# The norm of the short-conv heads: the same sums of squares taken in channel layout instead of token layout

## The chip, the cores and the metric

The kernel runs on one core of a Trainium2 chip. Its metric is the device time of one execution in microseconds. Five engines work side by side and meet at semaphores: PE (TensorE, matrix multiplies and transposes into PSUM), DVE (VectorE), ACT (ScalarE, functions from a loaded table), POOL (GpSimd), and SP, which only issues DMAs.

## The reference, cut to what matters

One layer of a hybrid encoder over 1024 tokens and 1024 channels, float32. The part that the change touches is the gated short convolution of the first 512 channels and its norm over 8 groups (heads) of 64 channels:

```
def group_rms_norm(y, g, n_groups):
    b, s, w = y.shape
    yf = y.astype(jnp.float32).reshape(b, s, n_groups, w // n_groups)
    yf = yf * lax.rsqrt(jnp.mean(yf * yf, axis=-1, keepdims=True) + EPS)
    return (yf.reshape(b, s, w) * g.astype(jnp.float32)).astype(y.dtype)
...
        y_conv = short_gated_conv(hc, bg, cg, w_conv[l])
        y_attn = chunked_band_attention(q, k, v, rel_bias[l])
        y = jnp.concatenate([group_rms_norm(y_conv, g_conv_out[l], CONV_GROUPS),
                             group_rms_norm(y_attn, g_attn_out[l], N_HEADS)], axis=-1)
        y = jnp.einsum('bsm,md->bsd', y, w_out[l])
```

Before it stand the pre-norm and the input projection, behind it a post-norm, the residual, and a SwiGLU feed-forward of width 2816 with norms of its own.

## The kernel before, in words

All matrix products are written out in "high" and "low" parts: ACT copies an operand to the fp32r type (high), DVE subtracts that from the original (low), and PE adds up high by high, high by low and low by high. The input projection of the first channels runs in six rounds ("front", `FRONT = 6`) of seven products each, by a scheme that trades one of eight block products for sums: `front_multiply(n, i)` is product i of round n, 12 matmuls of 512 columns. Its results meet in PSUM banks that DVE reads and adds up in a chain (`make_u2`, `make_u3`, `make_c22`, `make_c21`, `make_c12`), and product 6 writes into the bank that `make_c22` has just read. In the text "round 4, product 6" is `front_multiply(4, 6)`.

The conv output of channel block t (128 channels, two heads; t = 0 to 3) lies in channel layout: channels on the partitions, 1024 tokens along a row. Blocks 0 to 2 are normed during rounds 4 and 5 of the front, block 3 in the output projection (`down(c, ...)`, c = 0 to 7 its first pass). For each block the kernel does this:

- `square_y` / `square_conv` (ACT): the squares, into row CU.
- `conv_stats` (PE, line 1001): eight small fp32 matmuls, one for 128 tokens, with the squares as weights and a 128x2 matrix `group` of ones as columns, so that the sums of the two heads come out with the tokens on the partitions (128x16 in all).
- `conv_stats_read` (DVE, L2010), `conv_norm_factors` (POOL, a power of -1/2 on 128x16), `spread_conv` (ACT, L1467, each factor copied to 64 columns of row CR).
- `conv_norms` (PE, line 1007): eight transposes back to channel layout, and `conv_mix` / `conv_last` (DVE, L2015, L2336), which multiplies the row by them and by the gain.

Nothing reorders instructions: each engine runs its own list as written. PE's list of the front has a table `behind` that says behind which product a norm step comes. ACT's and DVE's lists of rounds 4 and 5 are written out by hand in the lines that follow `spread_conv` and `gated_round`. On SP, `store_conv(t)` waits for the finished row t, and the loads of later weights stand behind it. In the output projection DVE's table `tasks` puts `conv_last` into step c = 5, ahead of the split of the last operand row, which product c = 7 needs.

Of the kernel before, what the change touches and what calls it, by code (L numbers as in the profile page):

```python
# [48 lines left out]
def trunk_layer(nc, x, w_in, w_conv, rel_bias, g_conv_out, g_attn_out, w_out, g_pre_mix, g_post_mix,  # L49
# [71 lines left out]
    with ctx:  # L121
# [13 lines left out]
        arena_r = sb("arena_r", [P, NF * SEQ], F32R)  # L135
        misc = sb("misc", [P, 4 * BAND])
        ident = sb("ident", [P, P])
        group = sb("group", [P, 2])
        params = sb("params", [P, PAIRS, 5])
# [7 lines left out]
        var = sb("var", [P, 16])  # L147
# [95 lines left out]
        u2, u3, c22, s11, s4 = [misc[:, n * 512:(n + 1) * 512] for n in range(5)]  # L243
        s1, s2 = [o_raw[:, 4 * n:4 * n + 4, :].rearrange("p i c -> p (i c)") for n in range(2)]
# [159 lines left out]
        conv_factors = sem("conv_factors")  # L404
        conv_rs = sem("conv_rs")
        conv_stat = sem("conv_stat")
        conv_var = sem("conv_var")
# [4 lines left out]
        conv_norm = sem("conv_norm")  # L412
# [270 lines left out]
        def _(pool):  # L683
# [7 lines left out]
            nc.gpsimd.memset(group[0:HD, 0:1], 1.0).then_inc(consts_made, 1)  # L691
            pool.wait_ge(consts_made, 4)
            nc.gpsimd.memset(group[HD:P, 1:2], 1.0).then_inc(consts_made, 1)
            pool.wait_ge(consts_made, 5)

# [38 lines left out]
            def conv_norm_factors(t):  # L734

                pool.wait_ge(conv_var, t + 1)
                if t > 0:
                    pool.wait_ge(conv_rs, t)
                factors_to(crs[:, :], var[:, :], 16, conv_factors, t + 1)

# [4 lines left out]

            for t in range(PAIRS - 1):
                conv_norm_factors(t)
# [16 lines left out]
            conv_norm_factors(PAIRS - 1)  # L764

# [88 lines left out]
        def _(pe):  # L854
# [95 lines left out]
            def step(t, s):  # L950
# [16 lines left out]
                if s > 0:  # L967
                    pe.wait_ge(exp_done, unit(t, 2 * s))
                    if s in (2, 4):
                        pe.wait_ge(pT_act, tile(t, s - 1))  # L970
                    if s == 1 and t == 0:
                        pe.wait_ge(conv_mixed, PAIRS - 1)
# [23 lines left out]

            def conv_stats(bank):

                pe.wait_ge(consts_made, 5)
                for i in range(NT):  # L1000
                    last = mm(bank[:, 2 * i:2 * i + 2], row(CU, P, i * P), group[:, :], start=True, stop=True)  # L1001
                return last

            def conv_norms(bank, first, n):

                for b in range(n):
                    last = tr(bank[:, b * P:(b + 1) * P], row(CR, P, (first + b) * P), ident[:, :])  # L1007
                return last


# [107 lines left out]
            def stats(t):  # L1118

                pe.wait_ge(conv_sq, t + 1)  # L1120
                if t == 0:
                    pe.wait_ge(v_copied, NT)
                else:
                    pe.wait_ge(conv_var, t)
                conv_stats(PP[3]).then_inc(conv_stat, 1)

            def norms(t):

                pe.wait_ge(conv_rs, t + 1)
                if t > 0:  # L1130
                    pe.wait_ge(conv_mixed, t)
                conv_norms(PP[2], 0, NT).then_inc(conv_norm, 1)

            behind = {(4, 1): (stats, 0), (4, 3): (stats, 1), (4, 4): (norms, 0),
                      (5, 0): (norms, 1), (5, 1): (stats, 2), (5, 4): (norms, 2)}
            for n in range(FRONT):
                for i in FRONT_ORDER[n]:
                    front_multiply(n, i)
                    if (n, i) in behind:
                        task, t = behind[n, i]  # L1140
                        task(t)
# [57 lines left out]
            for c in range(len(PASSES) * KT):  # L1199
# [4 lines left out]
                if c == 3:  # L1204
                    pe.wait_ge(oT_read, PAIRS)
                    pe.wait_ge(conv_sq, PAIRS)
                    conv_stats(PP[3]).then_inc(conv_stat, 1)
# [6 lines left out]
                def begin(n, p=p):  # L1214
# [6 lines left out]
                    if p == 1 and n == 0:  # L1221
                        pe.wait_ge(mix_done, 1)
# [118 lines left out]
        def _(act):  # L1341
# [120 lines left out]
            def spread_conv(t):  # L1462

                act.wait_ge(conv_factors, t + 1)
                if 0 < t < LAST:
                    act.wait_ge(conv_norm, t)
                go(row(CR).rearrange("p (g d) -> p g d", d=HD),  # L1467
                   crs[:, :].rearrange("p (g o) -> p g o", o=1).broadcast_to([P, 16, HD]), ACT.Copy
                   ).then_inc(conv_rs, 1)
# [25 lines left out]
            front_copy_first(4), square_y(0)  # L1495
            front_high(5, 0), square_y(1), front_high(5, 1), front_high(5, 2), front_high(5, 3)
            spread_conv(0), front_high(5, 4), spread_conv(1), front_high(5, 6)
            front_copy_first(5), square_y(2), front_high(5, 5)
# [7 lines left out]
            first_chunk(0), spread_conv(2)  # L1506
# [191 lines left out]
            for c in range(1, NOUT):  # L1698
                if c < KT - 1:
                    split_out_w(c + 1), split_out_a(c + 1)  # L1700
                if c == 4:
                    act.wait_ge(oT_psum, PAIRS)
                    spread_conv(PAIRS - 1)
# [136 lines left out]
        def _(dve):  # L1840
# [165 lines left out]
            def conv_stats_read(t):  # L2006
                dve.wait_ge(conv_stat, t + 1)
                if t > 0:
                    dve.wait_ge(conv_factors, t)
                ts(var[:, :], PP[3][:, 0:16], 1.0 / HD, EPS, ALU.mult, ALU.add).then_inc(conv_var, 1)  # L2010

            def conv_mix(t):

                dve.wait_ge(conv_norm, t + 1)
                stt(row(CONV_ROWS[t]), PP[2], params[:, t, 3:4], row(CONV_ROWS[t]), ALU.mult, ALU.mult  # L2015
                    ).then_inc(conv_mixed, 1)
# [61 lines left out]
            conv_stats_read(0)  # L2078
# [6 lines left out]
            front_low(5, 3)  # L2085
            make_c22(4, tiles_of(row(CV), 1), 1)
            conv_stats_read(1)
            front_low(5, 4)
            make_c21(4, tiles_of(row(CV), 0), 0)
            conv_mix(0)  # L2090
# [3 lines left out]

            make_u2(5)
            conv_mix(1)
            make_u3(5)
            conv_stats_read(2)
            front_low(5, 5)
            low(1, 0, 0)  # L2100
            make_c22(5)
            conv_mix(2)
# [227 lines left out]
            def conv_last_stats(_):  # L2330
                dve.wait_ge(conv_stat, PAIRS)
                ts(var[:, :], PP[3][:, 0:16], 1.0 / HD, EPS, ALU.mult, ALU.add).then_inc(conv_var, 1)

            def conv_last(_):
                dve.wait_ge(conv_norm, PAIRS)
                stt(row(PAIRS - 1), PP[3], params[:, LAST, 3:4], row(CV), ALU.mult, ALU.mult).then_inc(mix_done, 1)  # L2336
# [8 lines left out]
            tasks = {1: [(attn_last, 0)], 3: [(conv_last_stats, 0)], 5: [(conv_last, 0)],  # L2345
# [303 lines left out]
```

## Time and profile before

| what | value |
|---|---|
| median of 3 runs | 1108.43 us (1108.36 to 1108.7) |
| the profiled execution | 1108.64 us |
| its span, first to last instruction | 1106.6 us |
| PE busy | 1096.3 us, 99% of the span |
| DVE busy | 769.2 us, 70% |
| ACT busy | 467.5 us, 42% |
| POOL busy | 160.5 us, 15% |

The profile is one execution taken by the hardware profiler; its own time is 2.0 us longer than its span. Busy times of PE are those of overlapping matmuls (one of 512 columns is recorded as 389 ns, and starts every 227 ns), so durations on PE are read as the distance from one start to the next.

### The profile page before, as it was taken

The page shows a single profiled execution, that of the slowest core. Times are in us where ns is not written, and L with a number is a line of the kernel's source. Part 1 is how long each engine was busy: PE and PEld are TensorE (multiplying, and loading weights), DVE is VectorE, ACT ScalarE, POOL GpSimd, SP SyncE. Part 2 cuts the span into 40 slices and gives each one's busy share as a digit, 9 for nine tenths or more (in the row PEclk, how much of TensorE's full clock was granted, in tenths as well). Part 3 has the DMA queues.
Part 4 walks back from the last instruction along what each step waited for, and adds up shares of the span by engine and source line. Part 5 has one row for each costly group of instructions (what it writes and reads, how often), then busy time and mean ns, then how long its engine had stood idle before and what let it go on. Part 6 is the DMA issues. An engine that isn't in the chain of part 4 may idle for free.

```text
span 1106.6 us, 16038 instructions
## 1 busy us (share of the span) xinstructions
PE 1096.3 (99%) x5653; PEld 907.9 (82%) x5653; DVE 769.2 (70%) x1270; ACT 467.5 (42%) x818; POOL 160.5 (15%) x258
## 2 busy tenths in 40 slices
PE   8999999999999999999999999999999999999997
PEld 7888887878888888888888888888888888888886
DVE  6878855455657656968787777878787777555584
ACT  6542233555555655734322232323223247444441
POOL 2300022010101220312112211211221110000031
PEclk9999999999999999999999999999999999999999
DMA  7332216300100444535546435543644689777632
GB/s 272 110 118 73 58 57 229 115 20 20 39 1 20 163 162 134 172 95 172 161 143 209 136 122 187 177 145 114 218 134 154 213 290 391 239 227 232 215 115 79
DMA packets 116182, 164.10 MB, mean 148 GB/s; under 512 B 7752, under 2 KB 73304, under 8 KB 116128
## 3 DMA queue, kind: packets, MB, share of 16 engines
q1 hardware_dynamic: 98496, 103.30, 29.2%
q0 software_dynamic: 16464, 55.89, 14.4%
q10 hardware_dynamic: 1168, 4.20, 1.0%
q8 instruction: 33, 0.54, 0.2%
q14 instruction: 21, 0.17, 0.0%
HBM read 119.56 MB, written 46.94 MB: 150 GB/s over the span
## 4 chain that ended last, share of the span: by engine, by line
PE 97%; ACT 1%; DVE 1%; DMA 1%; POOL 0%; issue 0%; SPq 0%; DVEq 0%; POOLq 0%
PE psum L1280 34%; PE psum L1307 18%; PE psum L874 12%; PE psum L1113 10%; PE psum L1164 8%; PE psum L1025 4%; PE psum L917 3%; PE psum L898 2%; PE psum L888 2%; PE psum L863 1%; PE psum L1001 1%; DMA arena<-in_x 1%; PE psum L925 0%; PE psum L1007 0%; PE psum L907 0%; ACT arena L1516 0%
## 5 line engine op out<-in xcount | busy, mean ns | idle before, releaser
L1280 PE MATMUL psum<-arena_r,ws 128*128 128x512 f32 x960 | 224.1, 389 | 0.0
L1280 PEld LDWEIGHTS psum<-arena_r,ws 128*128 128x128 f32 x960 | 180.2, 188 | 37.4
L1280 PE MATMUL psum<-hT,ws 128*128 128x512 f32 x720 | 169.9, 389 | 0.0
L1280 PEld LDWEIGHTS psum<-hT,ws 128*128 128x128 f32 x720 | 135.1, 188 | 28.0
L874 PE MATMUL psum<-hT,ws 128*128 128x512 f32 (+1 forms) x624 | 142.3, 380 | 0.4 <-ACT arena L1542 0.4
L1307 PE MATMUL psum<-hT 128*128 128x512 f32 (+1 forms) x600 | 135.2, 385 | 0.0
L1307 PEld LDWEIGHTS psum<-hT 128*128 128x128 f32 x600 | 111.3, 188 | 22.5
L874 PEld LDWEIGHTS psum<-hT,ws 128*128 128x128 f32 x624 | 107.9, 189 | 20.1 <-issue 0.8
L2411 DVE TENSOR_TENSOR misc<-misc,psum 128x512 f32<-128x512 f32 x100 | 68.5, 685 | 48.4 <-PE psum L1280 46.1
L1731 ACT ACTIVATE ws<-o_raw 128x512 fp32r<-128x512 f32 x40 | 25.1, 628 | 139.1 <-DVE o_raw L2389 138.6
L1164 PE MATMUL psum<-ws,hT 128*128 128x512 f32 x348 | 81.8, 393 | 0.0
L1307 PE MATMUL psum<-ws 128*128 128x512 f32 (+1 forms) x348 | 78.1, 382 | 0.0
L1164 PEld LDWEIGHTS psum<-ws,hT 128*128 128x128 f32 x348 | 64.5, 188 | 13.5 <-issue 0.4
L1307 PEld LDWEIGHTS psum<-ws 128*128 128x128 f32 x348 | 63.8, 188 | 12.6
L1731 ACT ACTIVATE ws<-raw 128x512 fp32r<-128x512 f32 x80 | 49.7, 623 | 39.7 <-PE psum L1280 39.3
L1113 PE MATMUL psum<-arena_r,ws 128*128 128x512 f32 x276 | 65.4, 391 | 0.0
L1113 PEld LDWEIGHTS psum<-arena_r,ws 128*128 128x128 f32 x276 | 51.4, 188 | 10.5
L2406 DVE TENSOR_TENSOR ws<-raw,ws 128x512 fp32r<-128x512 f32 x80 | 55.1, 690 | 6.6
L2485 DVE TENSOR_TENSOR hT<-arena,hT 128x512 fp32r<-128x512 f32 x62 | 40.1, 687 | 21.8 <-ACT hT L1778 21.4
L1778 ACT ACTIVATE hT<-arena 128x512 fp32r<-128x512 f32 x62 | 35.6, 624 | 38.6 <-PE psum L1307 29.8
L1357 ACT ACTIVATE misc<-arena 128x1024 bf16<-128x1024 f32 (+2 forms) x37 | 34.8, 941 | 40.3 <-DVE arena L2537 16.6
L1113 PE MATMUL psum<-hT,ws 128*128 128x512 f32 x216 | 51.2, 390 | 0.0
(264 smaller groups left out, 1563.3 us busy)
## 6 DMA issues: line engine op xcount, KB each, us to landing
raw<-in_w_ffn_in SPq DMA_DIRECT2D x44, 512.0 KB, 4.1
act_scratch<-arena POOLq DMA_DIRECT2D x77, 256.0 KB, 3.2
raw<-in_w_in SPq DMA_DIRECT2D x22, 512.0 KB, 3.8
arena<-in_w_ffn_out POOLq DMA_DIRECT2D x22, 512.0 KB, 5.7
arena<-act_scratch SPq DMA_DIRECT2D x38, 256.0 KB, 3.5
arena<-in_x SPq DMA_DIRECT2D x16, 512.0 KB, 6.4
raw<-in_w_out SPq DMA_DIRECT2D x16, 512.0 KB, 3.5
raw<-act_scratch SPq DMA_DIRECT2D x26, 256.0 KB, 3.4
```

Source lines behind the costliest of these rows:

```text
L874: last = mm(PP[pair][:, at:end] if to is None else to, w[wp], hT[:, hp, k, at:end], start=(k == 0 and (wp, hp) == (0, 0)), stop=(k == KT - ...
L1025: last = mm(v_bank(i), hT[:, hp, k, i * P:(i + 1) * P], v_weights(wp, k), start=(k == 0 and part == 0), stop=k == 7 and part == (1 if i < ...
L1113: last = mm(blocks(front_bank(n, i)), w[:, k * P:(k + 1) * P], b_operand(i, part, k), start=fresh_bank and k == 0 and w is hi and part == ...
L1164: last = mm(pair[:, half * 512:(half + 1) * 512], a, ws[:, slot, wp, half * 512:(half + 1) * 512], start=(first is not None and a is hi an ...
L1280: last = mm(blocks(bank), w[:, k * P:(k + 1) * P], b_operand(i, part, k), start=fresh_bank and k == 0 and w is hi and part == 0, stop=k == ...
L1307: last = mm(bank[:, at:end], a[:, n * P:(n + 1) * P], b[:, at:end], start=fresh_bank and a is ah and b is bh, stop=i == NP - 1 and a is al ...
L1357: go(dst, src, ACT.Square, scale=scale, accum_out=acc).then_inc(done[0], 1)
L1731: go(w_op(i)[0], w_raw[i], ACT.Copy).then_inc(w_hi, 1)
L1778: go(out_op(c, part)[0], raw_ring[c % RING][:, part * 512:(part + 1) * 512], ACT.Copy).then_inc(out_hi, 1)
L2406: tt(lo, w_raw[i], hi.bitcast(F32), ALU.subtract).then_inc(w_split, 1)
L2411: tt(out, a, bank, ALU.add).then_inc(made, 1)
L2485: tt(lo, raw_ring[c % RING][:, part * 512:(part + 1) * 512], hi.bitcast(F32), ALU.subtract).then_inc(out_split, 1)
```

## The change

The norm stays in channel layout. PE multiplies a 128x128 block matrix that holds 1/64 where row and column belong to one head by the squares, so that every channel of a head gets the head's mean, at its own place. For blocks 0 to 2 the squares are split in two fp32r parts (a high copy on ACT, a low part by subtraction on DVE), and the matmuls take both; for block 3 the matmuls are plain fp32, one for each head and half row. ACT takes the root of mean + EPS out of PSUM, DVE the reciprocal of a whole 128x1024 row, and one more DVE operation multiplies by gain and row. The read of the sums, the power on POOL, the spreading copy and the transposes go.

```
+        same_head = misc_r[:, 3 * 512:3 * 512 + P]
...
             def stats(t):
+                pe.wait_ge(conv_lo, t + 1)
                 if t > 0:
+                    pe.wait_ge(conv_root, t)
+                for half in range(2):
+                    for part in (CR, CU):
+                        last = mm(PP[2][:, half * HALF:(half + 1) * HALF], same_head, row_r(part)[:, half * HALF:(half + 1) * HALF],
+                                  start=(part == CR), stop=(part == CU))
+                last.then_inc(conv_stat, 1)
-            behind = {(4, 1): (stats, 0), (4, 3): (stats, 1), (4, 4): (norms, 0),
-                      (5, 0): (norms, 1), (5, 1): (stats, 2), (5, 4): (norms, 2)}
+            behind = {(FRONT - 2, 3): 0, (FRONT - 1, 0): 1, (FRONT - 1, 3): 2}
...
                 if c == 3:
                     pe.wait_ge(oT_read, PAIRS)
                     pe.wait_ge(conv_sq, PAIRS)
-                    conv_stats(PP[3]).then_inc(conv_stat, 1)
-                if c == 6:
-                    pe.wait_ge(conv_rs, PAIRS)
-                    conv_norms(PP[3], 0, NT).then_inc(conv_norm, 1)
+                    for half in range(2):
+                        for h in range(2):
+                            last = mm(PP[3][h * HD:(h + 1) * HD, half * HALF:(half + 1) * HALF],
+                                      group[:, h:h + 1].broadcast_to([P, HD]), row(CU, HALF, half * HALF))
+                    last.then_inc(conv_stat, 1)
...
+            def high_sq(t):
+                act.wait_ge(conv_sq, t + 1)
...
+                if t > 0:
+                    act.wait_ge(conv_mixed, t)
+                go(row_r(CR), row(CU), ACT.Copy).then_inc(conv_hi, 1)
+            def conv_roots(t, bank):
+                act.wait_ge(conv_stat, t + 1)
+                go(row(CR), bank, ACT.Sqrt, bias=eps_col[:, 0:1]).then_inc(conv_root, 1)
...
+            def low_sq(t):
+                dve.wait_ge(conv_hi, t + 1)
+                tt(row_r(CU), row(CU), row_r(CR).bitcast(F32), ALU.subtract).then_inc(conv_lo, 1)
+            def conv_mix(t, src, to):
+                dve.wait_ge(conv_root, t + 1)
+                chain(nc.vector.reciprocal(row(CR), row(CR)))
+                return stt(to, src, params[:, t, 3:4], row(CR), ALU.mult, ALU.mult)
+            def mix_row(t):
+                conv_mix(t, row(CONV_ROWS[t]), row(CONV_ROWS[t])).then_inc(conv_mixed, 1)
```

PE's list, rounds 4 and 5, before (L1113 is a product of the front, 128x2 the sums, ident the transposes):

```order
L1113 MATMUL psum<-arena_r,ws 128x512 x11
L1001 MATMUL psum<-group,arena 128x2 [waits consts_made,v_copied,conv_sq]
L1001 MATMUL psum<-group,arena 128x2 x7
L1113 MATMUL psum<-arena_r,ws 128x512 [waits c21_made,front_lo]
L1113 MATMUL psum<-arena_r,ws 128x512 x11
L1113 MATMUL psum<-hT,ws 128x512 [waits p1_copied,front_lo]
L1113 MATMUL psum<-hT,ws 128x512 x11
L1001 MATMUL psum<-group,arena 128x2 [waits consts_made,conv_var,conv_sq]
L1001 MATMUL psum<-group,arena 128x2 x7
L1113 MATMUL psum<-arena_r,ws 128x512 [waits c12_made,front_lo]
L1113 MATMUL psum<-arena_r,ws 128x512 x11
L1007 MATMUL psum<-ident,arena 128x128 [waits conv_rs]
```

The same place in the changed kernel, to the product that waits for `make_c22` (L1089 is the product, L1101 the matmuls with the block matrix):

```order
L1089 MATMUL psum<-arena_r,ws 128x512 [waits c21_made,front_lo]
L1089 MATMUL psum<-arena_r,ws 128x512 x11
L1089 MATMUL psum<-hT,ws 128x512 [waits p1_copied,front_lo]
L1089 MATMUL psum<-hT,ws 128x512 x11
L1101 MATMUL psum<-arena_r,misc_r 128x512 [waits conv_lo]
L1101 MATMUL psum<-arena_r,misc_r 128x512 x3
L1089 MATMUL psum<-arena_r,ws 128x512 [waits c12_made,front_lo]
L1089 MATMUL psum<-arena_r,ws 128x512 x11
L1089 MATMUL psum<-arena_r,ws 128x512 [waits u3_made,front_lo]
L1089 MATMUL psum<-arena_r,ws 128x512 x11
L1089 MATMUL psum<-hT,ws 128x512 [waits c22_made,front_lo]
```

The sums of block 0 have gone behind round 4's product 3, those of blocks 1 and 2 behind products 0 and 3 of round 5, and the groups of eight transposes are gone.

DVE's list at the end of round 4, before (L1996 multiplies a gate in, L1966 reads a bank, here for `make_c22` and `make_c21`, L1961 makes a low part):

```order
L1996 TENSOR_TENSOR arena<-arena,psum 128x4x128 [waits prod]
L1961 TENSOR_TENSOR ws<-raw,ws 128x512 [waits front_hi]
L1966 TENSOR_TENSOR arena<-misc,psum 128x4x128 [waits prod]
L2010 TENSOR_SCALAR var<-psum 128x16 [waits conv_factors,conv_stat,c22_made]
L1961 TENSOR_TENSOR ws<-o_raw,ws 128x512 [waits front_hi]
L1966 TENSOR_TENSOR arena<-misc,psum 128x4x128 [waits prod]
L2015 SCALAR_TENSOR_TENSOR arena<-psum,params,arena 128x1024 [waits conv_norm,c21_made]
```

And in the changed kernel:

```order
L1973 TENSOR_TENSOR arena<-arena,psum 128x4x128 [waits prod]
L1938 TENSOR_TENSOR ws<-raw,ws 128x512 [waits front_hi]
L1990 RECIPROCAL arena<-arena 128x1024 [waits conv_root]
L1991 SCALAR_TENSOR_TENSOR arena<-arena,params 128x1024 [waits dve_seq]
L1943 TENSOR_TENSOR arena<-misc,psum 128x4x128 [waits prod]
L1938 TENSOR_TENSOR ws<-o_raw,ws 128x512 [waits front_hi,c22_made]
L1985 TENSOR_TENSOR arena_r<-arena,arena_r 128x1024 [waits conv_hi]
L1943 TENSOR_TENSOR arena<-misc,psum 128x4x128 [waits prod]
```

The reciprocal of block 0 and its product with the row now stand ahead of the read for `make_c22`; before, the row was multiplied behind the read for `make_c21`.

ACT's list at the same place in the changed kernel (L1412 makes a high part, L1446 is the root, L1430 the square, L1441 the high copy of the squares):

```order
L1412 ACTIVATE ws<-raw 128x512 [waits prod,raw_landed0]
L1446 ACT_TABLE_LOAD
L1446 ACTIVATE arena<-psum,eps_col 128x1024 [waits conv_stat]
L1430 ACTIVATE arena<-arena 128x1024 [waits conv_stat,front_out]
L1412 ACTIVATE ws<-o_raw 128x512 [waits prod,s_made]
L1441 ACTIVATE arena_r<-arena 128x1024 [waits conv_mixed,conv_sq]
L1412 ACTIVATE ws<-misc 128x512 [waits prod,s_made]
```

Before, none of the table loads stood there, and the spreading copies of L1467 stood where the roots are. A fourth place is like the second: in the output projection the reciprocal of block 3 stands on DVE where L2336 stood, ahead of the two splits of step c = 6.

## Rows read from the trace of the kernel before

**Rows 1.** The page: busy time of PE, granted clock, the chain by engine.
```profile
PE 1096.3 (99%) x5653; PEld 907.9 (82%) x5653; DVE 769.2 (70%) x1270; ACT 467.5 (42%) x818; POOL 160.5 (15%) x258
...
PEclk9999999999999999999999999999999999999999
...
PE 97%; ACT 1%; DVE 1%; DMA 1%; POOL 0%; issue 0%; SPq 0%; DVEq 0%; POOLq 0%
```

**Rows 2.** Timeline of PE, rounds 3 to 5: start us, us, line, operation, count.
```profile
134.24 5.60 PE L1113 MATMUL psum<-hT,ws 128*128 128x512 f32 x24
139.68 2.88 PE L1113 MATMUL psum<-arena_r,ws 128*128 128x512 f32 x12
142.40 1.84 PE L1001 MATMUL psum<-group,arena 128*128 128x2 f32 x16
144.10 2.97 PE L1113 MATMUL psum<-arena_r,ws 128*128 128x512 f32 x12
...
183.47 2.88 PE L874 MATMUL psum<-hT,ws 128*128 128x512 f32 x12
```

**Rows 3.** Groups by line and shape, DVE: busy us, mean ns, idle us before.
```profile
L2140 DVE TENSOR_SCALAR nmax<-omax 128x1 f32<-128x1 f32 x64 | 9.8, 154 | 2.2
L2297 DVE TENSOR_TENSOR arena<-arena 128x1024 f32<-128x1024 f32 x8 | 9.8, 1224 | 0.3
...
L2593 DVE RECIPROCAL newt<-gate 128x1 f32<-128x1 f32 x1 | 0.2, 165 | 0.2 <-ACT gate L1816 0.2
...
L2591 DVE TENSOR_TENSOR newt<-ssq 128x1 f32<-128x1 f32 x1 | 0.2, 158 | 0.1
```

**Rows 4.** Timeline of ACT, round 4.
```profile
141.14 1.05 ACT L1460 ACTIVATE arena<-arena 128x1024 f32<-128x1024 f32 x1
142.09 0.62 ACT L1442 ACTIVATE ws<-raw 128x512 fp32r<-128x512 f32 x1
```

**Rows 5.** Timeline of ACT near the end: the one load of the root's table.
```profile
1085.56 1.28 ACT L1835 ACT_TABLE_LOAD   x1
1086.86 0.21 ACT L1835 ACTIVATE o_eps<-rst 128x4 f32<-128x4 f32 x1
```

**Rows 6.** Timeline of DVE, rounds 4 and 5.
```profile
142.67 0.69 DVE L1966 TENSOR_TENSOR misc<-misc,psum 128x512 f32<-128x512 f32 x1 [1.52 <-PE psum L1113]
...
147.84 0.69 DVE L1945 TENSOR_TENSOR o_raw<-raw 128x512 f32<-128x512 f32 x1
...
150.75 0.69 DVE L1961 TENSOR_TENSOR ws<-o_raw,ws 128x512 fp32r<-128x512 f32 x1
151.36 0.68 DVE L1961 TENSOR_TENSOR ws<-raw,ws 128x512 fp32r<-128x512 f32 x1
...
154.41 0.69 DVE L1966 TENSOR_TENSOR arena<-misc,psum 128x512 f32<-128x512 f32 x1 [1.17 <-PE psum L1113]
...
158.74 1.28 DVE L2015 SCALAR_TENSOR_TENSOR arena<-psum,params,arena 128x1024 f32<-128x1024 f32 x1
```

**Rows 7.** Timeline of PE in the output projection's first pass, and plain fp32 matmuls before it.
```profile
365.82 1.26 PE L917 MATMUL psum<-arena 128*64 128x128 f32 x20
...
380.65 1.84 PE L1001 MATMUL psum<-group,arena 128*128 128x2 f32 x16
382.35 12.55 PE L1164 MATMUL psum<-ws,hT 128*128 128x512 f32 x54
...
395.53 18.03 PE L1164 MATMUL psum<-ws,hT 128*128 128x512 f32 x78
```

**Rows 8.** Timeline of ACT there (L1636 copies an operand row, L1467 spreads factors).
```profile
385.38 1.04 ACT L1636 ACTIVATE hT<-arena 128x1024 fp32r<-128x1024 f32 x1
387.33 1.06 ACT L1467 ACTIVATE arena<-crs 128x1024 f32<-128x1024 f32 x1 [0.90 <-POOL crs L701]
```

**Rows 9.** Timeline of DVE there (L2280 makes an operand row's low part).
```profile
390.51 1.22 DVE L2280 TENSOR_TENSOR hT<-arena,hT 128x1024 fp32r<-128x1024 f32 x1
...
398.29 1.23 DVE L2280 TENSOR_TENSOR hT<-arena,hT 128x1024 fp32r<-128x1024 f32 x1
```

More of the change, by code:

```diff
@@ L135, in trunk_layer @@
         arena_r = sb("arena_r", [P, NF * SEQ], F32R)
+        with nc.sbuf_tensor("misc_r", [P, 4 * BAND], F32R) as misc_r:
+            pass
         misc = sb("misc", [P, 4 * BAND])
@@ L403, in trunk_layer @@
         conv_sq = sem("conv_sq")
[L404 to L405 removed]
+        conv_hi = sem("conv_hi")
+        conv_lo = sem("conv_lo")
         conv_stat = sem("conv_stat")
[L407 removed]
         o_var = sem("o_var")
@@ L744, in o_norm_factors @@
                 factors_to(rst[:, :], o_eps[:, :], UNITS, o_rs, t + 1)
-            for t in range(PAIRS - 1):
-                conv_norm_factors(t)
             pool.wait_ge(prod, multiplied(FRONT - 1, 4))
@@ L971, in step @@
                     if s == 1 and t == 0:
-                        pe.wait_ge(conv_mixed, PAIRS - 1)
+                        pe.wait_ge(conv_root, PAIRS - 1)
                     if s == 2 and t > 1:
@@ L995, in transpose_o @@
                 last.then_inc(oT_psum, 1)
[L997 to L1008, printed above, removed]
             def values(i, steps, part):
@@ L1139, in _ @@
                     if (n, i) in behind:
-                        task, t = behind[n, i]
-                        task(t)
+                        stats(behind[n, i])
             for q in range(AHEAD):
@@ L1460, in square_y @@
                 go(row(CU), row(CONV_ROWS[t]), ACT.Square).then_inc(conv_sq, 1)
[L1462 to L1469, printed above, removed]
+            def high_sq(t):
+                act.wait_ge(conv_sq, t + 1)
+                if t == 0:
+                    act.wait_ge(consts_made, 6)
+                    go(same_head.rearrange("p (g d) -> p g d", d=HD),
+                       group[:, :].rearrange("p (g o) -> p g o", o=1).broadcast_to([P, 2, HD]), ACT.Copy)
+                if t > 0:
[4 more added lines that the diff above has]
+                go(row(CR), bank, ACT.Sqrt, bias=eps_col[:, 0:1]).then_inc(conv_root, 1)
             scale = HD ** -0.5
@@ L1494, in _ @@
                 front_high(4, i)
[L1495 to L1498, printed above, removed]
+            front_copy_first(4), square_y(0), high_sq(0)
+            for i in range(4):
+                front_high(5, i)
+            conv_roots(0, PP[2]), square_y(1), front_high(5, 4), high_sq(1), front_high(5, 6)
+            front_copy_first(5), conv_roots(1, PP[2]), square_y(2), high_sq(2)
             def first_chunk(g):
@@ L2077, in _ @@
             front_low(5, 0)
-            conv_stats_read(0)
+            low_sq(0)
             make_u3(4)
@@ L2093, in _ @@
             times(2, 1, u2).then_inc(front_out, 1)
+            mix_row(1)
             make_u2(5)
-            conv_mix(1)
+            low_sq(2)
             make_u3(5)
-            conv_stats_read(2)
+            low(1, 0, 0)
             front_low(5, 5)
-            low(1, 0, 0)
+            mix_row(2)
             make_c22(5)
-            conv_mix(2)
             nc.vector.memset(gate[:, :], 0.0).then_inc(tile_free, 1)
@@ L2328, in low_t @@
                 dve.wait_ge(t_lo, 2 * m + 10)
-            def conv_last_stats(_):
-                dve.wait_ge(conv_stat, PAIRS)
-                ts(var[:, :], PP[3][:, 0:16], 1.0 / HD, EPS, ALU.mult, ALU.add).then_inc(conv_var, 1)
             def conv_last(_):
-                dve.wait_ge(conv_norm, PAIRS)
-                stt(row(PAIRS - 1), PP[3], params[:, LAST, 3:4], row(CV), ALU.mult, ALU.mult).then_inc(mix_done, 1)
+                conv_mix(LAST, row(CV), row(PAIRS - 1)).then_inc(mix_done, 1)
                 dve.wait_ge(mix_done, 1)
```

47 lines of the change are left out of this document (11 added, 36 removed).

## The prediction, made before the changed kernel had run

> **What bounds the kernel now.** I read the page first. The chain that ended last is 97% PE, and the granted clock stands at its upper level, 2.4 GHz, in every slice [rows 1]. So time that leaves PE's list is gained in full, if DVE and ACT keep up, and time that PE must wait is lost in full. Then I read the timelines of PE, ACT and DVE side by side in the two stretches that the change touches: rounds 4 and 5 of the front (142 to 184 us) and the first pass of the output projection (380 to 400 us).
>
> **What PE saves.** Twelve products of the front run between the first sums of squares at 142.40 and the next stage at 183.47 [rows 2]. Two products take 139.68 - 134.24 = 5.44, so one takes 2.72, and a matmul of 512 columns 0.227. Twelve make 32.64; the 41.07 between the two starts hold 8.43 of norm work (three groups of sums, of 144.10 - 142.40 = 1.70 each, three of transposes, and small gaps). Instead come three times four fp32r matmuls of 512 columns, the same form as the products': 12 x 0.227 = 2.73. Saved in the front: 5.70.
>
> In the output projection the sums take 382.35 - 380.65 = 1.70 [rows 7]. Product c = 7 starts 18 matmuls behind 395.53, at 399.61. Without norm work, c = 3 to 6 are 72 x 0.227 = 16.32. The four plain fp32 matmuls that come are twice two output halves of 64 partitions. The nearest row is L917, the same M = 64, K = 128 and fp32: ten such matmuls of 128 columns (two records each) in 1.26, so 0.126 each [rows 7]; four of 512 columns are 16 x 0.126 = 2.0. From below it is the fp32r price, 0.9; from above double, 4.0, if the two halves of the output, which alternate in both places, overlap there and not here. I take 2.0: c = 7 is wanted at 380.65 + 2.0 + 16.32 = 398.97, a saving of 0.64. All told PE's list is 6.3 shorter.
>
> **The unknown: the reciprocal of a 128x1024 row, R.** Four of them are new on DVE. The trace has one reciprocal, of a single column: 165 ns, against 158 for a product or sum of two columns and 154 (mean of 64) for one input and a constant [rows 3]. Rows of 1024 take 1224, that is 1.04 a column above the first. From below, then, R = 1.2, if the 7 ns are a fixed cost. If they belong to the element, it takes 1.04 + 7 = 8.0 ns, and R = 0.16 + 1024 x 8.0 ns = 8.4. Measured against 154 it would be 11 ns more, 12.0 an element and R = 12.4, the upper end. I take 8.4: 7 ns are almost seven of DVE's steps of 1.04, which an operation that streams as the others do has no reason to need, and the 64 runs of the one-column form say that such a duration is steady. This step decides the result.
>
> The Trainium skill speaks on both sides. VectorE: DVE Perf Modes, First, the fixed hardware budget, says that the reciprocal divides iteratively, on two slices with a repeat count of 8; that read as eight steps for an element would give an estimate of 1024 x 8 / 0.96 GHz = 8.5, and the one-column row agrees. Vector Engine (DVE) Microarchitecture Reference, Anatomy of a single slice, has the chain of divisions span all eight slices; that read as a pipeline is the first rival below.
>
> **Walk through the front, with R open.** Small latencies of a semaphore are taken as 0.06. *First block.* ACT squares until 142.19 [rows 4], expands the block matrix (0.25, my estimate from a 512 column copy's 0.62), copies high until 143.45 and makes the next operand's high part. DVE, from 142.67 [rows 6], does u2, a low part (0.61 from 150.75 to 151.36), the low squares (1.2), u3, and the four sums (2.91 from 147.84 to 150.75), which now end near 149.5. The block's means run on PE from 147.84 to 148.75. ACT still has three high parts, the first behind the third sum: until 150.4. Then the root's table is loaded, 1086.86 - 1085.56 = 1.30 [rows 5], and the root of 1024 columns takes 1.03, near the square's 1.05: 152.74. On DVE the low parts and the gate product end at 151.9. So the reciprocal starts at 152.8, the product with gain and row takes 1.28 (L2015's duration), the read for c22 0.69 [rows 6]: c22 is made at 154.77 + R. Before, it was made at 155.1, early enough that PE shows no idle time before round 4's product 6, which waits for it. Now that product is wanted at 142.40 + 4 x 2.72 + 0.91 = 154.19. **Wait 1: R + 0.64.** It exists even at R = 1.2, because the whole pair now stands ahead of a bank read that PE waits for.
>
> *Second block.* Its high copy waits on ACT for the first row (conv_mixed), with one high part of round 5 queued behind, no more. After product 6 and product 0 come the means, 0.91, the root, the second reciprocal and the product, the high copy 1.05 and low squares 1.2 of the third block: made at 165.98 + 2R. PE wants them at 169.34 + R. **Wait 2: R - 3.3**, if positive.
>
> *Third block.* Means until 166.94 + 2R, a high part and the root, 1.7, the reciprocal, 1.28, and c22 of round 5 at 170.68 + 3R, against 172.39 + 2R when its product 6 is wanted. **Wait 3: R - 1.65.** Queued behind on DVE are only the last low parts of q and k, and these end before the three pieces of the next projection do. SP holds back one weight load behind the second row's store; that row is done at 163.6 + 2R, and the load is first used behind round 5's product 4, at 169.7 + 2R: 6 us of room, whatever R is. POOL's powers leave the chain. The load of the exponential's table falls into ACT's idle time before the first scores, at nothing; if that cover went, 1.3.
>
> *Output projection.* ACT ends the copy that starts at 385.38 near 386.34 [rows 8], loads the table (1.30), takes the root (1.03): 388.67, and two more copies. DVE's low part, at 390.51 before, ends at 392.0 instead of 391.7 [rows 9]. Then R, 1.28, and two splits of a row, 2.4 together, of which the second, at 398.29 before, is what product c = 7 waits for: done at 395.7 + R. **Wait 4: R - 3.3.**
>
> The Trainium skill (ScalarE: Activation LUTs, What ACT_TABLE_LOAD costs) adds a drain of some 1.38 to each table switch, 2.66 in all. The trace has the next instruction 1.30 behind the load's start [rows 5], so it does not agree and I keep 1.30; by the page wait 1 and wait 4 would each grow by up to 1.4.
>
> **The sum.** -6.3 + (R + 0.64) + (R - 3.3) + (R - 1.65) + (R - 3.3), brackets not below zero. With R = 8.4: -6.3 + 9.0 + 5.1 + 6.75 + 5.1 = +19.7. Zero change is at R = 3.4.
>
> One more price appears in waits this long. PE stands at the upper clock throughout [rows 1] and is hardly ever idle, so no row shows what it does after 9 us of idleness. If the granted clock falls to 1.2 GHz, the first product behind a wait takes 5.44 instead of 2.72 [rows 2]: bounds 0 and 4 x 2.7 = 10.9. I take one product, 2.7, for the longest wait. Total +22.4. The profiled execution took 1108.64, 0.2 more than the median of the runs; 1108.6 + 22.4 = 1131.0.
>
> **Rivals.**
> - *Fast reciprocal.* The 7 ns are fixed and R = 1.2. For it: all other DVE forms of 1024 columns take 1.2 to 1.3. Against it: that excess in an operation of one column. Only wait 1 is left, 1.84: -6.3 + 1.84 = -4.5, so 1104.1. It decides for faster below R = 3.4. This is the microarchitecture page's chain through all slices, worked out from rows.
> - *A reciprocal in between*, R = 3 to 4.2, two or three cycles a column: -1.3 to +3.1, so 1107.3 to 1111.7. Nothing in a row speaks for it but the coarse reading of 7 ns.
> - *A slow reciprocal at a lower price*, part of the slow case: if part of the 7 ns is fixed, R = 6.0 gives +10.1, or 1118.7. *At a higher price*, R = 9.5 and all four waits followed by half clock, 24.1 + 10.9 = 35, or 1143.6.
> - *The saving is hidden anyway.* If another limit held the front (loads, or the scores' start), PE's gain would vanish even with R = 1.2: 1108. Against it: PE idles nowhere in the two stretches.
>
> **How the numbers follow.** Slow reciprocal 0.77, with its own range 1117 to 1143; fast 0.14; in between 0.06; hidden 0.03. The predicted time is the slow case's, 1131.0. The range of 8 in 10 has to leave out no more than the fast case and the tails: 1109 to 1142. Faster by over 0.2% (2.2 us, about what a measurement can tell from no change) 0.15: the fast case and a little of the next. Within 0.2%: 0.06. Slower: 0.79.
>
> **What would show it.** RECIPROCAL of 128x1024 near 8.4 us, four times, DVE's busy time up by about 37 (33.6 and three low squares of 1.2). PE idle before round 4's product 6 of some 9 us, before the third means of 5, before round 5's product 6 of 7, and before c = 7 of 5. The means as three groups of 0.9 on PE; the last as 2.0. A reciprocal below 3.4 us makes the forecast wrong in sign; waits of that size with another releaser than DVE make its reasons wrong; a granted clock that stays at 2.4 GHz takes the 2.7 away.

## The result, and the profile after

The changed kernel takes 1126.64 us (median of 4 runs, 1126.08 to 1127.14) against 1108.51 us for the kernel before on the same chip (4 runs): 1.0163 times as long, 95% interval 1.015 to 1.0175. So it is slower by 18.1 us; 1131.0 was predicted, with 1109 to 1142 as the range. The profiled execution has a span of 1125.4 us, 18.8 more than before.

The page of the changed kernel, the lines that answer to [rows 1]:

```profile
PE 1098.1 (98%) x5577; PEld 905.6 (80%) x5577; DVE 798.3 (71%) x1273; ACT 475.0 (42%) x825; POOL 147.4 (13%) x255
...
PEclk9999988999999999999999999999999999999999
...
PE 92%; DVE 4%; ACT 2%; DMA 1%; issue 1%; DVEq 0%; SPq 0%; POOL 0%; ACTq 0%; POOLq 0%
```

The chain that ended last has 5 points less of PE, and DVE and ACT have gained 3 and 1: it now runs through both. In slices 6 and 7 (141 to 197 us) the granted clock's digit is 8 instead of 9; before, it was 9 in every slice [rows 1].

The groups of DVE by line and shape (busy us, mean ns, idle before; answers to [rows 3]):

```profile
L1990 DVE RECIPROCAL arena<-arena 128x1024 f32<-128x1024 f32 x4 | 26.2, 6552 | 5.0 <-ACT arena L1446 5.0
L1991 DVE SCALAR_TENSOR_TENSOR arena<-arena,params 128x1024 f32<-128x1024 f32 x4 | 5.1, 1284 | 0.1
L1985 DVE TENSOR_TENSOR arena_r<-arena,arena_r 128x1024 fp32r<-128x1024 f32 x3 | 3.7, 1220 | 0.7 <-ACT arena_r L1441 0.7
```

The reciprocal takes 6.55 us, five times a product or sum of the same row, and not 8.4. Its 26.2 us and the 3.7 of the low squares are the 29.1 us by which DVE's busy time has grown, to within 0.8.

The timeline of PE in rounds 4 and 5 (start, us, line, operation, count, the idle time before in brackets; L1101 are the head means; answers to [rows 2]):

```profile
147.92 1.07 PE L1101 MATMUL psum<-arena_r,misc_r 128*128 128x512 f32 x4
148.83 5.60 PE L1089 MATMUL psum<-arena_r,ws 128*128 128x512 f32 x24
161.58 8.55 PE L1089 MATMUL psum<-hT,ws 128*128 128x512 f32 x24 [7.15 <-DVE arena L1943]
169.97 1.07 PE L1101 MATMUL psum<-arena_r,misc_r 128*128 128x512 f32 x4
170.88 5.60 PE L1089 MATMUL psum<-arena_r,ws 128*128 128x512 f32 x24
176.32 2.88 PE L1089 MATMUL psum<-hT,ws 128*128 128x512 f32 x12
182.63 2.07 PE L1101 MATMUL psum<-arena_r,misc_r 128*128 128x512 f32 x4 [3.44 <-DVE arena_r L1985]
184.50 4.59 PE L1089 MATMUL psum<-arena_r,ws 128*128 128x512 f32 x12
188.94 2.90 PE L1089 MATMUL psum<-arena_r 128*128 128x512 f32 x12
195.09 4.50 PE L1089 MATMUL psum<-hT,ws 128*128 128x512 f32 x12 [3.25 <-DVE misc L1943]
199.43 2.89 PE L865 MATMUL psum<-hT,ws 128*128 128x512 f32 x12
```

Read the starts. The 24 matmuls from 148.83 are due to end at 154.27, and product 6 starts at 161.58: wait 1, 7.3 us. The 12 from 176.32 are due to end at 179.04, and the means start at 182.63: wait 2, 3.6. The 12 from 188.94 are due to end at 191.66, and product 6 starts at 195.09: wait 3, 3.4. The other thing to see is how long the work behind each wait takes. The 24 matmuls behind wait 1 take 169.97 - 161.58 = 8.39, where 24 at the upper clock take 176.32 - 170.88 = 5.44; behind wait 2 four take 1.87 instead of 0.91 and twelve 4.44 instead of 2.72; behind wait 3 twelve take 4.34.

The windows of the same stretch show why (length; busy us of PE, PEld, DVE, ACT and POOL; granted clock; DMA share, GB/s):

```profile
150.00:160.00 10.00, 4.43 (x20) 3.35 (x18) 9.06 (x6) 4.36 (x5) 0.00 (x0) 0.87 0.18 52
160.00:165.00 5.00, 3.42 (x8) 2.77 (x9) 4.55 (x6) 1.58 (x2) 0.00 (x0) 0.50 0.26 105
165.00:170.00 5.00, 5.00 (x18) 3.92 (x18) 1.38 (x2) 0.00 (x0) 0.00 (x0) 0.74 0.00 0
170.00:180.00 10.00, 9.20 (x41) 7.29 (x39) 7.74 (x2) 2.66 (x3) 0.00 (x0) 1.00 0.00 0
180.00:190.00 10.00, 7.37 (x21) 5.86 (x22) 7.97 (x7) 4.12 (x5) 0.60 (x1) 0.66 0.31 105
190.00:200.00 10.00, 6.75 (x24) 5.13 (x23) 8.49 (x10) 2.32 (x3) 1.37 (x4) 0.83 0.91 294
```

160 to 165 us, around the end of wait 1, stands at 0.50 throughout, the lower level (1.2 GHz). The means of 0.66 and 0.83 hold the falls at waits 2 and 3. Between waits 1 and 2 the clock is back at 1.00 (170 to 180), and so it is behind wait 2 (1.00 from 190 to 194).

DVE and ACT around wait 1 (answers to [rows 6] and [rows 4, 5]):

```profile
152.96 6.55 DVE L1990 RECIPROCAL arena<-arena 128x1024 f32<-128x1024 f32 x1 [0.91 <-ACT arena L1446]
159.55 1.28 DVE L1991 SCALAR_TENSOR_TENSOR arena<-arena,params 128x1024 f32<-128x1024 f32 x1
160.75 0.68 DVE L1943 TENSOR_TENSOR arena<-misc,psum 128x512 f32<-128x512 f32 x1
```

```profile
150.52 1.28 ACT L1446 ACT_TABLE_LOAD   x1
151.81 1.12 ACT L1446 ACTIVATE arena<-psum,eps_col 128x1024 f32<-128x1024 f32 x1
```

The reciprocal and the product stand ahead of the bank read (L1943) that product 6 waits for. The reciprocal starts at 152.96, forecast as 152.8; the root starts 1.29 behind the start of its table load.

The output projection's first pass on PE and on DVE (answers to [rows 7] and [rows 9]):

```profile
397.02 1.94 PE L1178 MATMUL psum<-arena,group 128*64 128x512 f32 x8
398.89 16.66 PE L1133 MATMUL psum<-ws,hT 128*128 128x512 f32 x72
418.47 13.85 PE L1133 MATMUL psum<-ws,hT 128*128 128x512 f32 x60 [2.92 <-DVE hT L2258]
432.16 1.04 PE L854 MATMUL psum<-ident,arena 128*128 128x128 f32 x8
```

```profile
408.04 6.55 DVE L1990 RECIPROCAL arena<-arena 128x1024 f32<-128x1024 f32 x1
...
417.09 1.23 DVE L2258 TENSOR_TENSOR hT<-arena,hT 128x1024 fp32r<-128x1024 f32 x1
```

The fourth reciprocal holds up the split (L2258) that c = 7 needs. The plain fp32 matmuls take 398.89 - 397.02 = 1.87. The 60 matmuls behind this wait take 13.69, 0.228 each: here the clock did not fall.

The span's 18.8 us, from starts on PE:

| part | us |
|---|---|
| PE's list in rounds 4 and 5 is shorter | -5.7 |
| waits 1, 2, 3: 7.31 + 3.59 + 3.43 | +14.3 |
| work behind them at the lower clock: 2.95 + 0.96 + 1.72 + 1.62 | +7.25 |
| so the next stage starts at 199.43 instead of 183.47 (0.1 was late already) | +16.0 |
| from there to the sums of block 3 (397.02 against 380.65, less 15.96) | +0.4 |
| from there to c = 7 (418.47 against 399.61, less 16.37) | +2.5 |

### The profile page after: what moved, and what is told of

Read it like the earlier page. It is cut to its first block, busy times and chain, and to the rows that moved or that the text cites. A ratio compares the mean times of both kernels' runs of the same rounds, so it can differ in the third digit from the quotient of the medians.

```text
span 1125.4 us, 15886 instructions
## 1 busy us (share of the span) xinstructions
PE 1098.1 (98%) x5577; PEld 905.6 (80%) x5577; DVE 798.3 (71%) x1273; ACT 475.0 (42%) x825; POOL 147.4 (13%) x255
## 3 DMA queue, kind: packets, MB, share of 16 engines
q0 software_dynamic: 16464, 55.89, 14.3%
## 4 chain that ended last, share of the span: by engine, by line
PE 92%; DVE 4%; ACT 2%; DMA 1%; issue 1%; DVEq 0%; SPq 0%; POOL 0%; ACTq 0%; POOLq 0%
PE psum L1250 34%; PE psum L1277 18%; PE psum L865 12%; PE psum L1089 9%; PE psum L1133 6%; PE psum L1001 4%; PE psum L908 3%; PE psum L889 2%; DVE arena L1990 2%; PE psum L879 2%; PE psum L854 1%; DMA arena<-in_x 1%; DVE ws L1833 0%; PE psum L916 0%; ACT arena L1446 0%
## 5 line engine op out<-in xcount | busy, mean ns | idle before, releaser
L1250 PE MATMUL psum<-hT,ws 128*128 128x512 f32 x720 | 169.9, 389 | 0.0
L1250 PEld LDWEIGHTS psum<-hT,ws 128*128 128x128 f32 x720 | 135.1, 188 | 28.0
L865 PEld LDWEIGHTS psum<-hT,ws 128*128 128x128 f32 x624 | 107.9, 189 | 20.0 <-issue 0.8
L1089 PE MATMUL psum<-arena_r,ws 128*128 128x512 f32 x276 | 66.1, 396 | 0.0
L1089 PE MATMUL psum<-hT,ws 128*128 128x512 f32 x216 | 55.8, 415 | 10.4 <-DVE arena L1943 7.2
L1089 PEld LDWEIGHTS psum<-arena_r,ws 128*128 128x128 f32 x276 | 53.2, 193 | 11.3
L1089 PEld LDWEIGHTS psum<-hT,ws 128*128 128x128 f32 x216 | 43.4, 203 | 21.3 <-issue 11.2
L1327 ACT ACTIVATE misc<-arena 128x1024 bf16<-128x1024 f32 (+2 forms) x37 | 34.8, 941 | 40.1 <-DVE arena L2510 16.6
```

The costliest lines, as they stand in the source:

```text
L865: last = mm(PP[pair][:, at:end] if to is None else to, w[wp], hT[:, hp, k, at:end], start=(k == 0 and (wp, hp) == (0, 0)), stop=(k == KT - ...
L1089: last = mm(blocks(front_bank(n, i)), w[:, k * P:(k + 1) * P], b_operand(i, part, k), start=fresh_bank and k == 0 and w is hi and part == ...
L1250: last = mm(blocks(bank), w[:, k * P:(k + 1) * P], b_operand(i, part, k), start=fresh_bank and k == 0 and w is hi and part == 0, stop=k == ...
L1327: go(dst, src, ACT.Square, scale=scale, accum_out=acc).then_inc(done[0], 1)
```

## Experiments

The theory of the prediction is *length*: DVE's reciprocal is long, and as it stands ahead of four operations that PE waits for, it costs its length less some slack. Its rivals: the wait belongs to ACT's tables and roots, or to the order of DVE's list rather than to the length. A second question is whether the lower clock is a cost of its own, or only a mark of the waiting.

**A product in the reciprocal's place.** The norm comes out without its reciprocal.

```
-                chain(nc.vector.reciprocal(row(CR), row(CR)))
+                chain(tt(row(CR), row(CR), row(CR), ALU.mult))
```

> The changed kernel with each of the four reciprocals replaced by a product of the row with itself (so the norm is not what the reference asks for). Every wait, table load and matmul stays. Theory (the price of the reciprocal, 6.55 us a row in the changed kernel's trace, and the half clock after the waits that it makes): with R = 1.2 only the wait before round 4's product 6 stays, about 1.8 us; the sum of the prediction gives -4.5 against the kernel before, 1104 us, and a clock that never falls. Rival (the new queue order and the two table loads in the stretch, whatever the arithmetic costs): waits stay above 3 us, the time stays above 1115 us.

Measured: 1104.9 us (7 runs, 1104.49 to 1106.5), 0.9971 of before (0.996 to 0.9983). All else of the change stays, its tables, roots and order, and it is over 3 us faster than before. PE's timeline:

```profile
156.02 7.33 PE L1089 MATMUL psum<-hT,ws 128*128 128x512 f32 x24 [1.83 <-DVE arena L1943]
163.20 1.07 PE L1101 MATMUL psum<-arena_r,misc_r 128*128 128x512 f32 x4
```

Of the four waits only wait 1 is left, 1.83 us, near what the fast rival of the prediction said (1.84). (The figure in brackets is some 0.16 shorter than a wait counted from starts: wait 1 of the changed kernel is 7.15 by the bracket and 7.31 by the starts.) Yet the 24 matmuls behind it take 7.18 instead of 5.44: the clock fell at a wait of 1.8 us. The seven executions differ in the clock too: the four of 1104.5 to 1104.9 have a mean granted clock of 0.999, the three of 1106.2 to 1106.5 one of 0.997 or 0.998. The profiled one, 1106.16, is of the second kind.

**The reciprocal of half the row.** The second half of each row keeps the plain root.

```
-                chain(nc.vector.reciprocal(row(CR), row(CR)))
+                chain(nc.vector.reciprocal(row(CR, HALF), row(CR, HALF)))
```

> The changed kernel with the reciprocal of the first 512 columns of each row only (the other half keeps the root, so the output is not the reference's). Theory (about 6.25 ns for each column): RECIPROCAL of 128x512 takes 3.35 us. By the prediction's sum, -6.3 + 4.0 + 0.05 + 1.7 + 0.05 = -0.5, so 1108 us, no change within 1 us if the clock holds; if it falls behind the wait of 4 us, up to 3 us more. Rival (a large fixed part in the 6.55): the operation takes over 4.5 us and the time is over 1112 us.

Measured: 1110.87 us (10 runs), 1.0024 of before (1.0015 to 1.0034), with reciprocals of 3.35 us. PE waits 4.0, 0.2 and 1.7 in the front, as R + 0.64, R - 3.3 and R - 1.65 give, and loses 1.70 behind the first. With R = 3.35 the forecast's sum is -0.5; the measured medians are 2.4 apart (1110.87 and 1108.48), and the next stage starts at 186.18, 2.7 later than before. The 1.70 of slower work is the largest part of the 2.9 between sum and measurement: the clock turns what the sum calls no change into a loss.

**The price of a reciprocal.** Six of different shapes, one behind the other, are added on DVE behind the last work of the kernel before; their results are not used.

> The kernel before with six reciprocals added on DVE behind its last work, on rows that nothing reads: 128x1024, 128x512, 128x128, 64x512, 128x512 out of PSUM, 128x16. Theory (6.25 ns, six cycles of 0.96 GHz, for each column, and some 0.15 us fixed): 6.55, 3.35, 0.95, 3.35, 3.35 and 0.26 us. Rival 1 (eight cycles a column and part of it hidden by something in the row form): 4.3 us for 512 columns. Rival 2 (a price that depends on partitions or on the memory read): the 64x512 and the PSUM form differ from the plain 128x512 by over 10%.

Measured: 1124.5 us, one execution; only the six durations are read from it. The groups of DVE by shape:

```profile
L2628 DVE RECIPROCAL misc<-misc 128x1024 f32<-128x1024 f32 x1 | 6.5, 6544 | 0.0
L2632 DVE RECIPROCAL misc<-psum 128x512 f32<-128x512 f32 x1 | 3.4, 3357 | 0.0
L2629 DVE RECIPROCAL misc<-misc 128x512 f32<-128x512 f32 x1 | 3.4, 3353 | 0.0
L2631 DVE RECIPROCAL misc<-misc 64x512 f32<-64x512 f32 x1 | 3.3, 3345 | 0.0
L2630 DVE RECIPROCAL misc<-misc 128x128 f32<-128x128 f32 x1 | 1.0, 953 | 0.0
L2633 DVE RECIPROCAL misc<-misc 128x16 f32<-128x16 f32 x1 | 0.3, 253 | 0.0
```

(6544 - 3353) / 512 = 6.23 ns a column, (3353 - 953) / 384 = 6.25, (953 - 253) / 112 = 6.25, and about 0.15 us that does not grow. It is the same from PSUM and on half the partitions. So one column's cost is 6.25, where the forecast took 8.0. That is six of DVE's steps of 1.04 [rows 3].

**PE kept busy in the waits.** 30, 14 and 20 matmuls of which nobody reads the result are put ahead of the three operations that wait.

```
+            def busy(n):
+                for _ in range(n):
+                    mm(PP[3][:, 0:HALF], hT[:, 0, 0, 0:P], hT[:, 0, 0, 0:HALF], start=True, stop=True)
+            fill = {(FRONT - 2, 6): 30, (FRONT - 1, 6): 20}
...
+                        if (n, i) == (FRONT - 1, 3):
+                            busy(14)
                         stats(behind[n, i])
```

> The changed kernel with 30, 14 and 20 matmuls on constant data added on PE where it waited: ahead of round 4's product 6, of the third block's means, and of round 5's product 6 (6.8, 3.2 and 4.5 us of 7.3, 3.6 and 3.4 to 4.9 us of waiting). They write a bank that nothing reads. Theory (the granted clock falls to 1.2 GHz because PE idled, and that costs on the path 2.95 behind wait 1, 0.96 for the means and 1.6 behind wait 3): the clock stays at 2.4 GHz in the front and the time falls by about 5.5 us, to 1121 us. Rival (the clock falls for another reason, or the slower matmuls were hidden behind DVE's chain): 1126 us or more.

Measured: 1123.49 us (4 runs, 1121.68 to 1124.96), 1.0139 of before (1.0122 to 1.0156). PE's timeline (L1107 are the added matmuls, L1952 is the bank read in this version):

```profile
154.28 6.96 PE L1107 MATMUL psum<-hT 128*128 128x512 f32 x30
161.59 5.72 PE L1089 MATMUL psum<-hT,ws 128*128 128x512 f32 x24 [0.35 <-DVE arena L1952]
167.15 1.07 PE L1101 MATMUL psum<-arena_r,misc_r 128*128 128x512 f32 x4
...
186.30 4.70 PE L1107 MATMUL psum<-hT 128*128 128x512 f32 x20
191.40 3.00 PE L1089 MATMUL psum<-hT,ws 128*128 128x512 f32 x12 [0.40 <-DVE misc L1952]
194.24 4.24 PE L865 MATMUL psum<-hT,ws 128*128 128x512 f32 x18
```

Product 6 starts at 161.59, as in the changed kernel: the added work did not delay it. But the next 24 take 5.56 instead of 8.39, and the next stage starts 5.2 us earlier. So the lower clock is a cost of its own, some 5 us of the 18. Not all of its 7.25 was lost: with the clock up, PE comes earlier to wait 3, which is now 191.40 - 186.30 = 5.10 instead of 3.43, so what PE lost on product 4 in the changed kernel came out of wait 3.

The profiled execution is one of the two shorter ones (1121.68 and 1122.04, mean granted clock 0.999); the other two took 1124.94 and 1124.96 at 0.995, so by the medians the gain is 3.15 us. Where the clock fell in those two no record shows.

**The reads ahead of the reciprocals.** In rounds 4 and 5 DVE does `make_c22` before the row.

```
             front_low(5, 3)
-            mix_row(0)
             make_c22(4, tiles_of(row(CV), 1), 1)
             front_low(5, 4)
+            mix_row(0)
...
-            mix_row(2)
             make_c22(5)
+            mix_row(2)
```

> The changed kernel with DVE's list in another order: the bank reads make_c22 of rounds 4 and 5 (and one low part) ahead of the reciprocals of blocks 0 and 2. Theory (the length of the chain root, reciprocal, row, next block's high and low squares sets the front, the queue position only a part of it): PE's waits move to the means of blocks 1 and 2, 5.6 us each in a walk with R = 6.55, and wait 3 goes; the front is 4.3 us shorter, so about 1122 us, or 1 to 2 us less still if the shorter waits keep the clock up. Rival (the queue position alone costs the time): waits 1 and 3 go and nothing takes their place, 1112 us or less. Other rival: no change, 1126 us, the waits are all given back.

Measured: 1127.56 us (4 runs), 1.0173 of before (1.0156 to 1.019): nothing gained. PE's timeline:

```profile
165.30 2.08 PE L1101 MATMUL psum<-arena_r,misc_r 128*128 128x512 f32 x4 [5.54 <-DVE arena_r L1985]
...
180.03 2.07 PE L1101 MATMUL psum<-arena_r,misc_r 128*128 128x512 f32 x4 [3.48 <-DVE arena_r L1985]
...
190.62 4.24 PE L865 MATMUL psum<-hT,ws 128*128 128x512 f32 x18
199.62 0.67 PE L879 MATMUL psum<-ws 64*128 64x256 f32 x6 [4.75 <-DVE ws L2091]
...
393.96 1.94 PE L1178 MATMUL psum<-arena,group 128*64 128x512 f32 x8
...
415.78 16.78 PE L1133 MATMUL psum<-ws,hT 128*128 128x512 f32 x60 [3.30 <-DVE hT L2258]
432.40 1.04 PE L854 MATMUL psum<-ident,arena 128*128 128x128 f32 x8
```

The expectation missed: it had the front 4.3 us shorter and all of that kept, some 1122 us; the time is the one of its last rival, that everything is given back. In the front waits 1 and 3 are gone, the means of blocks 1 and 2 wait 5.54 and 3.48, and the next stage starts 8.8 us earlier than in the changed kernel. Then the lead is given back. The third reciprocal now stands ahead of a split for the scores, and PE waits 4.75 at 199.62. The six matmuls behind that wait, at the lower clock, take 2.86, where the changed kernel's take 1.60. At 393.96 the lead is 3.1 us. In the output projection nearly the same wait (3.30 for 2.92) is now followed by the lower clock: 60 matmuls take 16.6 instead of 13.7, and the lead is gone. So with a reciprocal of 6.55 us the order of DVE's list only chooses who waits for it.

**The last block alone.** The kernel before, with only block 3 in the new form (plain fp32 means, root, reciprocal in `conv_last`).

```
                 if c == 3:
-                    conv_stats(PP[3]).then_inc(conv_stat, 1)
-                if c == 6:
-                    conv_norms(PP[3], 0, NT).then_inc(conv_norm, 1)
+                    for half in range(2):
+                        for h in range(2):
+                            last = mm(PP[3][h * HD:(h + 1) * HD, half * HALF:(half + 1) * HALF],
+                                      group[:, h:h + 1].broadcast_to([P, HD]), row(CU, HALF, half * HALF))
```

> The kernel before with only the last block's norm done in the new way (in the output projection): two 64-row fp32 matmuls for each half, root with a table load, reciprocal of 128x1024, no transposes. Theory (the changed kernel's trace read piece by piece): PE's list is 0.6 shorter, wait 4 before product c = 7 is 2.9 to 3.2 us, no fall of the clock; +2.5 us against before, 1111 us, so that the other three blocks are worth +15.6. Rival (the fall of the clock and the later shifts come from the front, and the last block alone is hidden): within 1 us of before.

Measured: 1112.82 us (5 runs, 1111.17 to 1114.49), 1.0043 of before (1.0029 to 1.0057). PE's timeline in the profiled execution, which is the one of 1111.17:

```profile
402.21 7.99 PE L1165 MATMUL psum<-ws,hT 128*128 128x512 f32 x34 [2.96 <-DVE hT L2283]
```

c = 7 starts at 402.21 instead of 399.61, +2.6, the tail's share in the table above; its 34 matmuls run at the upper clock. The mean granted clock of the five executions goes down as the time goes up: 0.999 for 1111.17 and 1111.98, 0.998 for 1112.82, 0.995 for 1113.8 and 1114.49. The profile caught an execution in which the clock stayed up behind a wait of 3.0 us. In others it fell somewhere, and the time is up to 3.3 us longer; that it fell behind this same wait is likely, as it is the only long one added, but no record shows it.

**One pass on ACT.** The table function that gives 1/sqrt takes the place of the root, and the reciprocal goes.

```
-                go(row(CR), bank, ACT.Sqrt, bias=eps_col[:, 0:1]).then_inc(conv_root, 1)
+                go(row(CR), bank, ACT.Abs_reciprocal_sqrt, bias=eps_col[:, 0:1]).then_inc(conv_root, 1)
...
-                chain(nc.vector.reciprocal(row(CR), row(CR)))
```

> The changed kernel with root and reciprocal replaced by one ACT pass, the table function 1/sqrt(|x|), and no reciprocal on DVE. Its accuracy is the table's. Theory: R = 0, the wait before round 4's product 6 is 0.6 us, no other wait; the prediction's sum gives -5.6, 1103 us. It beats before and after. Rival (the function is slower than a root on ACT, or needs a table load in each block): over 1106 us.

Measured: 1103.06 us (4 runs, 1102.91 to 1103.3), 0.9951 of before (0.9934 to 0.9967). The group on ACT, then PE's timeline:

```profile
L1446 ACT ACTIVATE arena<-psum,eps_col 128x1024 f32<-128x1024 f32 x4 | 4.5, 1113 | 0.3 <-PE psum L1101 0.3
```

```profile
154.91 5.69 PE L1089 MATMUL psum<-hT,ws 128*128 128x512 f32 x24 [0.54 <-DVE arena L1943]
...
178.57 3.79 PE L865 MATMUL psum<-hT,ws 128*128 128x512 f32 x16
```

The pass costs what the root cost (1113 ns in the changed kernel too). Wait 1 is down to 0.54, the other three are gone, and the clock stays up.

**One pass, and the reads first.** The last version with the order of DVE's list from the run before it.

> The kernel of e7_one_pass, and DVE's bank reads make_c22 of rounds 4 and 5 ahead of the products with rows 0 and 2. Theory: the last wait of 0.6 us in the front goes, or moves to the means of block 1 at under 0.5 us: 0.3 to 0.7 us less than e7_one_pass, 1102.5 us. Rival (wait 1 was hidden behind the next product's operands anyway): the same as e7_one_pass within 0.2 us.

Measured: 1102.21 us (4 runs, 1101.94 to 1102.26), 0.9942 of before (0.9926 to 0.9959): the best version, 6.3 us faster than before.

```profile
177.60 4.24 PE L865 MATMUL psum<-hT,ws 128*128 128x512 f32 x18
```

PE has no wait in rounds 4 and 5, and the next stage starts 183.47 - 177.60 = 5.87 us earlier than before. Of this, 0.16 was there ahead of any norm work: the means of block 0 start at 147.68 where 142.40 + 2 x 2.72 = 147.84 was due. What is left, 5.71, is the saving on PE's list in the front, with no wait on top of it; 5.70 was worked out. The whole gain, 6.3 us, is the forecast's saving on PE's list (6.3).

## Why the prediction was right, and where its sizes were off

The mechanism held: a long reciprocal on DVE stands ahead of what PE waits for, at the four places named.

- **PE's list.** Forecast 5.70 shorter in the front and 0.64 in the output projection. Shown: 5.71 in the run without waits; the fp32 means take 1.87, where 2.0 was taken. Right.
- **R, the step that decided.** Taken as 8.4, measured 6.55. The sum has 4R, so this term was 7.4 us too high. The inference that an excess of 7 ns in one column belongs to the element was right in kind. But it was read from a difference of two durations, and the same one-column reciprocal reads 164 or 162 ns in the other traces, where 165 stood. By 162 the forecast's rule gives 1.04 + 4 = 5.0 ns a column and R = 5.3. The true excess over a column of 1.04 is 5.2 ns. So the kind was read from the rows, and that the size came as near as it did is partly luck. The Trainium skill (VectorE: DVE Perf Modes, First, the fixed hardware budget) gives a repeat count of 8 for this division, which the prediction read as eight steps and an estimate of 8.5 us; the trace has 6.25 ns, or six steps, and the measurement decides. The chain of divisions that the Trainium skill has through all eight slices (Vector Engine (DVE) Microarchitecture Reference, Anatomy of a single slice), read as a pipeline at the others' 1.04 ns a column, does not agree with the reciprocals here.
- **Waits.** With R = 6.55 the forecast's own terms are 7.2, 3.25, 4.9 and 3.25; measured 7.3, 3.6, 3.4 and 2.9. Wait 3 is shorter because PE came to it late: product 4, ahead of it, had lost 1.72 to the lower clock. The run with PE kept busy and the half rows bear the terms out.
- **The clock.** The forecast took 2.7, one slow product behind the longest wait. It is 7.25 us of slower work behind three waits; some 5 of it reach the end. This term was half of what it is, and the choice of the longest wait alone was wrong: waits of 3.6 and 3.4 us were followed by it too, and in another version one of 1.8.
- **The sum.** The forecast's +22.4 loses 7.4 for R. It gains 2.8 for the clock (5.5 instead of 2.7), 0.7 for the waits of the front, 0.4 in the attention stage, and loses 0.1 in the tail: 18.8, the span's difference. (The 0.7 is 7.31 + 3.59 + 5.15 against 7.19 + 3.25 + 4.9, where 5.15 is wait 3 with the 1.72 that PE came late.) So two errors of opposite sign partly cancel, and that the total came within 4.4 us is in part luck; with R known and all else as it was, the forecast would have been 1123.6, 3.0 too low. By its own terms (4R - 13.9 once all four waits exist) zero change is at R = 3.5 rather than 3.4, R = 4.2 gives +2.9 rather than +3.1, and the upper end that it named, R = 12.4, would give +35.7, more than its range allowed for.
- **ACT.** The root takes 1.12, taken as 1.03; the table load 1.28, with the next operation 1.29 behind its start. The Trainium skill (ScalarE: Activation LUTs, What ACT_TABLE_LOAD costs) puts a drain of 1.38 on top; as in [rows 5], no load in the changed kernel shows it. The exponential's load stayed in idle time.
- **Rivals.** The fast reciprocal fell by its duration, though its price was right: with 1.2 us in that place, wait 1 is 1.83 and the time 1104.9, where 1104.1 was worked out. That the saving is hidden anyway fell with the one-pass runs, which keep it. That ACT's tables and roots are the cause, and not the reciprocal, fell with the product in its place.

## What to carry to other kernels

Before a function of one column is moved to whole rows, measure it at two widths: the fixed cost hides the price of an element, and here the sign of the forecast hung on 7 ns between two records. An engine that is only 70% busy can still hold up the busiest one, where a long operation stands ahead of something that the busiest engine waits for. Here reordering only chose who waits; a cheaper operation is what helped. And put on each new wait of PE not only its length but the slower work behind it.

## What the hardware showed that was not expected

- A reciprocal on DVE costs 6.25 ns a column and 0.15 us, whatever the partitions (64 or 128) and the source (SBUF 3353 ns, PSUM 3357 ns for 512 columns).
- The granted clock fell to its lower level at a PE wait of only 1.8 us (24 matmuls in 7.18 instead of 5.44). There it was 1.00 until 156 us, 0.70 from 156 to 158 and 0.50 from 158 to 160, so it fell only after PE had started again at 156.02; at wait 1 of the changed kernel it fell while PE was idle (0.50 from 158 to 160). Yet in the profiles of the changed kernel and of the last block alone it did not behind waits of 2.9 and 3.0 us. Behind 3.3 us at the same place it did, in the run with the reads first. Executions of one kernel differ in it: the mean granted clock goes down as the time goes up, by 1.7 us between the two kinds in the first experiment and by up to 3.3 in that of the last block. What decides it stays open.
- ACT's function for 1/sqrt takes 1.11 us for 128x1024 out of PSUM, no longer than the root.
